# Query and key units of the first mixer: products of 512 columns into two PSUM banks, halves added by VectorE

## The chip, the cores and the metric

One core of one Trainium2 chip runs the whole program. The metric is device time in microseconds (us), the median of several executions; lower is better. Besides these there is one execution recorded by the hardware profiler, from which all rows below come.

## The reference, cut to what matters

The program computes two transformer blocks on 256 tokens of width 1024, in float32. The first is a gated feed-forward, then a mixer, then a second gated feed-forward. The mixer projects its normed input `u` with one wide matrix and splits the columns:

```python
z, xbc, dt_raw, q, k, v, gate_logits = jnp.split(u @ w_in[l], IN_SPLITS, axis=-1)
y_ssd = ssd_branch(z, xbc, dt_raw, ...)      # a chunked scan: 4 groups, 2 chunks of 128 tokens
y_att = diff_attn_branch(q, k, v, ...)       # 8 heads of 2 x 64
merged = gates[:, :, 0] * y_ssd + gates[:, :, 1] * y_att
```

The change concerns the products for `q` and `k` alone (1024 columns each). What is computed stays the same.

## The kernel before, in words

**Precision by parts.** Every float32 product is made of three products of "round" parts. A weight unit is split into an upper part WH (ScalarE, `split_hi`, L487) and a lower part WL = weights - WH (VectorE, `split_lo`, L1082). The input rows are split likewise: XT holds, for each of 8 blocks of 128 input features (`k`), the upper part of the 256 tokens (XTH) and beside it the lower part (XTL), so that `XT[:, k]` is 512 columns. `parts` (L1797) issues WH x XTH, WL x XTH and WH x XTL, all added into one PSUM region.

**Units.** Weights come in units of 128 x 2048 values through a ring of 5 slots, loaded by the SyncE queue, which waits for TensorE to be done with the unit 5 earlier (`w_used`). One query or key unit is 256 columns of the weight. Its 256 output features are the PSUM rows, as two blocks `f` of 128 features, and the 256 tokens the columns. `channels` (L1803) makes for each `f` and `k` three products of 256 columns, 48 in a unit, and both blocks lie in one bank of 512 columns. ScalarE copies that bank to QK (L765). There are 8 such units: 0 to 3 are queries, 4 to 7 keys. The text calls them u0 to u7. They are followed by 4 units for `v` (u8 to u11, rows of tokens, products of 512 columns) and the first gate units (u12, u13).

**Banks.** PSUM has 8 banks: ACC is banks 0 to 3, TOP banks 4 to 7. u0 goes to bank 0, u1 to u7 in turn to 4 and 5 (`q_bank`, L374). Bank 2 takes the C x B products of the scan, bank 3 its outputs, bank 6 its states.

**The order around the change** is written out by hand. The scan runs in steps r = 0 to 8 (loops at L2080 for TensorE, L1406 for VectorE, L776 for ScalarE), and units are put between its products: one unit a step, two in steps 2, 4, 6 and 8 (`beside`, L345). u0 stands before the loop.

- TensorE in step r: the product C x B (L2086), then, from r = 1, the state product (L2098 or L2101) and the 8 output products of the step before (L2104), which wait for VectorE's decay matrix of that step (`ssd_m`, L2102), then the step's units (`qkv`, L2060). So u1 is in step 0, u2 in step 1, u3 and u4 in step 2, u5 in step 3, u6 and u7 in step 4, u8 in step 5. Unit n (n >= 2) waits until unit n-2 is out of its bank (`qkv_kept`, L2068).
- VectorE in step r: scaled inputs XDT (L1414) and in even steps XDEC (L1416), waiting for TensorE's outputs of the step before (`ssd_y`); the sums and the gating of Y (L1423 to L1430); the masked product CBM (L1433); the decay matrix times CBM (L1437), which TensorE awaits; then a wait for ScalarE's row factors (`y_rms`, L1439) and the normed output (L1440); then the step's `split_lo`, one or two.
- ScalarE in step r: 8 Relu and one Exp for the next decay matrix (L783, L786), the state copy (L791), the square of Y after VectorE's L1430 and L1437 (L794), Ln and Exp (L499, L500), then for each unit of the step a `split_hi` and the copy of that unit to QK (L765).

**The same scheme elsewhere.** The feed-forward's gate and up units are already computed as the change does it: `block` (L1865) makes 8 products WH x XT of 512 columns (L1870) and 8 products WL x XTH of 256 columns (L1873) into the right half of the same bank. ScalarE copies the right halves of two banks (L540), and VectorE adds the left halves (L1133).

Of the kernel before, what the change touches and what calls it, by code (L numbers as in the profile page):

```python
# [7 lines left out]
ALU = mybir.AluOpType  # L8
ACT = mybir.ActivationFunctionType
# [6 lines left out]
P = 128  # L16
D = 1024
KD = D // P
NT = 2
TOK = NT * P  # L20
# [169 lines left out]
def program(nc, w, out):  # L190
    with ExitStack() as ctx:
# [83 lines left out]
        def head_sm(q):  # L275
# [34 lines left out]
        end_half, last_half = sem("last_unit_first_columns"), sem("last_rows_halves")  # L310
        conv_1, conv_done, conv_silu, x_turned, x_kept = map(
            sem, ("conv_first_tap", "conv_done", "conv_silu", "x_turned", "x_kept"))
        dt_raw, z_kept, qkv_kept = map(sem, ("dt_raw", "z_kept", "qkv_kept"))
        dt_low, dt_sum, dt_turned, beside_lo = map(sem, ("dt_low_kept", "dt_sum", "dt_turned", "beside_unit_half"))
        cum_kept, cum_stored, cum_spread = sem("cum_rows_kept"), sem("cum_rows_stored"), [
            sem(f"cum_rows_spread{n}") for n in range(2)]
# [54 lines left out]
        def z_bank(n, t):  # L371
            return (2 if n == 1 else 4) + t

        def q_bank(n):  # L374
            return 5 - n % 2 if n else 0

        def v_bank(n, t):
            return ((0, 1), (7, 5))[n][t]


        def slot(c):
            return c % RING
# [99 lines left out]
        def _(act):  # L482
# [271 lines left out]
            def qkv(u):  # L754
                n = u - U_QKV
                split_hi()
                if n == 13:
                    for t in range(NT):
                        chunk_tile(U_GATE0, U_GATE0 + 1, t)
                        nc.scalar.activation(BUF1[:, t, 0:512], PS[gate_bank(0, t)][:], ACT.Copy).then_inc(gate0_kept, 1)  # L760
                elif n == 12:
                    pass
                elif n < 8:
                    act.wait_ge(w_used, u + 1)
                    nc.scalar.activation(QK[:, 2 * (n % 4):2 * (n % 4) + 2, n // 4, :],  # L765
                                         PS[q_bank(n)][:].rearrange("p (f t) -> p f t", f=2),
                                         ACT.Copy).then_inc(qkv_kept, 1)
                elif n % 2:
                    for t in range(NT):
                        chunk_tile(u - 1, u, t)  # L770
                        nc.scalar.activation(V[:, t, (n - 9) * 256:(n - 7) * 256], PS[v_bank(n // 2 - 4, t)][:],
                                             ACT.Copy).then_inc(qkv_kept, 1)

            qkv(U_QKV)
            u = U_QKV + 1
# [300 lines left out]
        def _(dve):  # L1076
# [5 lines left out]
            def split_lo():  # L1082

                c = next(splits, None)
                if c is None:
                    return
                s, n = slot(c), WIDTH.get(c, UNIT)
                dve.wait_ge(w_hi, c + 1)
                tt(WL[:, s, 0:n], RAW[:, s, 0:n], WH[:, s, 0:n].bitcast(F32), ALU.subtract).then_inc(w_lo, 1)  # L1089
# [312 lines left out]
            def heads_bc(ap):  # L1402
                return ap.unsqueeze(2).to_broadcast([P, HPG, SSD_P])

            split_lo()
            for r in range(9):  # L1406
                if r < 8:
                    g, c = divmod(r, 2)
                    xs = BUF1[:, c, g * GW:(g + 1) * GW]
                    hs = slice(c * 32 + g * HPG, c * 32 + (g + 1) * HPG)  # L1410

                    if r:
                        dve.wait_ge(ssd_y, r)
                    own.link(tt(by_head(XDT), by_head(xs), heads_bc(DT[:, 2, hs]), ALU.mult))  # L1414
                    if c == 0:
                        tt(by_head(XDEC), by_head(XDT), heads_bc(EX[:, 1, c, g * HPG:(g + 1) * HPG]),  # L1416
                           ALU.mult).then_inc(xdec_ok, 1)
                if r:
                    n = r - 1
                    g, c = divmod(n, 2)  # L1420
                    dve.wait_ge(skip_ok, r)
                    dve.wait_ge(ssd_y, r)
                    own.link(tt(Y, PS[3][:], Y, ALU.add))  # L1423
                    if c:
                        dve.wait_ge(ssd_st, r)
                        own.link(tt(by_head(T1), by_head(PS[6][:]),
                                    heads_bc(EX[:, 0, c, g * HPG:(g + 1) * HPG]), ALU.mult))
                        own.link(tt(Y, Y, T1, ALU.add))
                    zs = BUF2[:, c, g * GW:(g + 1) * GW]
                    tt(Y, Y, zs, ALU.mult).then_inc(y_gated, 1)  # L1430
                if r < 8:
                    dve.wait_ge(ssd_cb, r + 1)
                    tt(CBM[:], PS[2][:, 0:P], UPTO, ALU.mult).then_inc(ssd_cbm, 1)  # L1433
                    dve.wait_ge(ssd_cbm, r + 1)
                    dve.wait_ge(ssd_e, r + 1)
                    E = DECAY[r % 2]
                    tt(E, E, CBM[:].unsqueeze(1).to_broadcast([P, HPG, P]), ALU.mult).then_inc(ssd_m, 1)  # L1437
                if r:
                    dve.wait_ge(y_rms, r)  # L1439
                    stt(zs, Y, RS[:, 4:5], GAIN[:, g0(n) * GW:(g0(n) + 1) * GW], ALU.mult, ALU.mult).then_inc(ys_ok, 1)  # L1440
                else:
                    def g0(n):
                        return n // 2
                for _u in range(beside(r)):
                    if r == 8 and _u:
                        kt_lo(0)
                    split_lo()


            slopes = [2.0 ** (-8.0 * (h + 1) / DA_HEADS) for h in range(DA_HEADS)]  # L1450
# [254 lines left out]
        def _(pe):  # L1705
# [97 lines left out]
            def channels(c, bank, between=None):  # L1803

                s = slot(c)
                pe.wait_ge(w_lo, c + 1)
                for f in range(2):
                    if f and between:
                        between()
                    for k in range(KD):  # L1810
                        ws = slice(k * 256 + f * P, k * 256 + (f + 1) * P)
                        ins = parts(PS[bank][:, f * TOK:(f + 1) * TOK], WH[:, s, ws], WL[:, s, ws],
                                    XTH[:, k, :], XTL[:, k, :], k == 0, k == KD - 1)
                ins.then_inc(w_used, 1)
# [245 lines left out]
            def qkv(u):  # L2060
                n = u - U_QKV
                if n < 8:
                    if n == 0:
                        pe.wait_ge(conv_done, 11)
                    elif n == 1:
                        pe.wait_ge(z_kept, 8)
                    else:
                        pe.wait_ge(qkv_kept, n - 1)  # L2068
                    channels(u, q_bank(n))
                elif n % 2 == 0:  # L2070
                    v = n // 2 - 4
                    first_half(u, (v_bank(v, 0), v_bank(v, 1)), lambda t: pe.wait_ge(qkv_kept, 7) if v else pe.wait_ge(conv_done, 12))
                else:
                    second_half(u, (v_bank(n // 2 - 4, 0), v_bank(n // 2 - 4, 1)))

# [4 lines left out]
            for r in range(9):  # L2080
                if r < 8:
                    g, c = divmod(r, 2)
                    if r:
                        pe.wait_ge(ssd_cbm, r)

                    mm(PS[2][:, 0:P], BT[:, g, c * P:(c + 1) * P], CT[:, g, c * P:(c + 1) * P], start=True,  # L2086
                       stop=True).then_inc(ssd_cb, 1)
                if r:
                    n = r - 1
                    g, c = divmod(n, 2)  # L2090

                    if n:
                        pe.wait_ge(y_gated, n)
                    pe.wait_ge(cums_exp, 1)
                    pe.wait_ge(cum_cols, 1)
                    if c == 0:
                        pe.wait_ge(xdec_ok, n // 2 + 1)
                        mm(PS[6][:], B0[:, g * P:(g + 1) * P], XDEC, start=True, stop=True).then_inc(ssd_st, 1)  # L2098
                    else:
                        pe.wait_ge(state_ok, n // 2 + 1)  # L2100
                        mm(PS[6][:], CT[:, g, P:TOK], STATE, start=True, stop=True).then_inc(ssd_st, 1)  # L2101
                    pe.wait_ge(ssd_m, r)  # L2102
                    for e in range(HPG):
                        ins = mm(PS[3][:, e * SSD_P:(e + 1) * SSD_P], DECAY[n % 2][:, e, :], XDT[:, e * SSD_P:(e + 1) * SSD_P],  # L2104
                                 start=True, stop=True)
                    ins.then_inc(ssd_y, 1)
                for _u in range(beside(r)):
                    if u < U_GATE0:
                        qkv(u)
                    elif u == U_GATE0:  # L2110
                        first_half(u, (4, 0), lambda t: pe.wait_ge(qkv_kept, 8 + t))
                        pe.wait_ge(qkv_kept, 12)
                        turn_rows(0, BUF2, 0)
                    else:
                        second_half(u, (4, 0))
                    u += 1
# [324 lines left out]
```

## Time and profile before

| what | us |
|---|---|
| runs (3): median, lowest, highest | 1111.6, 1111.05, 1112.52 |
| the profiled execution's own time | 1111.03 |
| its span, first to last instruction | 1109.3 |
| stretch from u0 to the last step of the scan | 318.5 to 421 of the span |
| granted TensorE clock, mean | 1.000 |

All times in rows are us from the start of the span, and durations in them are us unless marked ns. PE is TensorE's products, PEld its weight loads, DVE VectorE, ACT ScalarE. Products overlap: one of 256 columns has a duration of 0.28 and the next begins 0.12 later, so what a stretch of TensorE work costs is read from starts.

### The profile page before, as it was taken

To read this page: it belongs to the slowest core of one execution; us is meant where nothing else is said; L and a number is where in the kernel's file an instruction comes from. 1 tells how busy PE (TensorE), PEld (TensorE's weight loads), DVE (VectorE), ACT (ScalarE), POOL (GpSimd) and SP (SyncE) were. 2 spreads that over 40 slices of the span, in tenths; PEclk is the share of its full clock that TensorE was granted. 3 is DMA by queue.
4 is the path that set the end of the run, shared out by engine and by line. 5 is a ranking of instruction groups with operands and counts; after the bars stand their busy time and mean duration, and the time that the engine had idled before them with its cause. 6 is when DMAs were issued, how large, how long until landed. Compare 5 with 4: busy or idle time off the path is not lost.

```text
span 1109.3 us, 14767 instructions
## 1 busy us (share of the span) xinstructions
PE 1094.5 (99%) x6036; PEld 934.9 (84%) x6036; DVE 770.2 (69%) x896; ACT 619.2 (56%) x883; POOL 36.5 (3%) x66
## 2 busy tenths in 40 slices
PE   7999999999999999999999999999999999999997
PEld 6888888899999987788888888888977778888886
DVE  5766667587767778868768666675784577766664
ACT  7544445564577756655455454456776636444443
POOL 0000000000001100000000000000021100000000
PEclk9999999999999999999999999999999999999999
DMA  9755554755566545345465555545643445555550
GB/s 314 250 192 189 190 191 151 237 168 195 181 189 201 172 152 209 122 155 198 163 219 190 192 188 190 191 150 179 208 137 131 171 152 190 190 189 190 190 190 38
DMA packets 131666, 202.27 MB, mean 182 GB/s; under 512 B 5088, under 2 KB 98144, under 8 KB 131344
## 3 DMA queue, kind: packets, MB, share of 16 engines
q1 hardware_dynamic: 127920, 189.56, 52.2%
q0 software_dynamic: 2672, 10.65, 2.8%
q10 hardware_dynamic: 1008, 1.12, 0.3%
q8 instruction: 48, 0.79, 0.3%
q14 instruction: 18, 0.15, 0.0%
HBM read 200.24 MB, written 1.08 MB: 181 GB/s over the span
## 4 chain that ended last, share of the span: by engine, by line
PE 91%; DVE 4%; ACT 3%; DMA 1%; issue 1%; ACTq 0%; DVEq 0%
PE TOP L1870 20%; PE ACC L1799 13%; PE ACC L1801 13%; PE ACC L1800 13%; PE TOP L1873 10%; PE TOP L1799 4%; PE TOP L1801 4%; PE TOP L1800 4%; ACT WH L494 1%; DVE WL L1089 1%; PE ACC L2104 1%; PE TOP L1715 1%; DMA RAW<-in_w_in 1%; PE TOP L1938 0%; PE TOP L2278 0%
## 5 line engine op out<-in xcount | busy, mean ns | idle before, releaser
L1089 DVE TENSOR_TENSOR WL<-RAW,WH 128x2048 fp32r<-128x2048 f32 (+3 forms) x177 | 400.0, 2264 | 112.5 <-ACT WH L494 111.9
L494 ACT ACTIVATE WH<-RAW 128x2048 fp32r<-128x2048 f32 (+1 forms) x179 | 337.6, 1890 | 80.4 <-DMA RAW<-in_ffn_w_gate 29.4
L1870 PE MATMUL TOP<-XT,WH 128*128 128x512 f32 x960 | 239.9, 392 | 0.0
L1870 PEld LDWEIGHTS TOP<-XT,WH 128*128 128x128 f32 x960 | 174.3, 189 | 32.4
L1799 PE MATMUL ACC<-WH,KTH 128*128 128x512 f32 (+1 forms) x452 | 178.7, 395 | 0.9 <-DVE KTL L1661 0.8
L1800 PE MATMUL ACC<-WL,KTH 128*128 128x512 f32 (+1 forms) x452 | 175.7, 389 | 0.0
L1801 PE MATMUL ACC<-WH,KTL 128*128 128x512 f32 (+1 forms) x452 | 175.6, 389 | 0.0
L1873 PEld LDWEIGHTS TOP<-XT,WL 128*128 128x128 f32 x960 | 131.0, 190 | 9.4
L1873 PE MATMUL TOP<-XT,WL 128*128 128x256 f32 x960 | 133.8, 282 | 0.0
L540 ACT ACTIVATE SCR<-TOP 128x512 f32<-128x512 f32 x60 | 35.8, 597 | 160.4 <-PE TOP L1873 160.4
L1799 PEld LDWEIGHTS ACC<-WH,KTH 128*128 128x128 f32 x452 | 85.0, 188 | 18.3 <-DVE KTL L1661 1.3
L1801 PEld LDWEIGHTS ACC<-WH,KTL 128*128 128x128 f32 x452 | 84.8, 188 | 17.9
L1800 PEld LDWEIGHTS ACC<-WL,KTH 128*128 128x128 f32 x452 | 85.1, 188 | 15.3
L1133 DVE TENSOR_TENSOR SCR<-TOP,SCR 128x512 f32<-128x512 f32 x60 | 41.4, 691 | 74.5 <-ACT SCR L540 74.5
L1799 PE MATMUL TOP<-WH,XT 128*128 128x512 f32 (+1 forms) x184 | 74.1, 403 | 2.3 <-DVE WL L1295 1.9
L1801 PE MATMUL TOP<-WH,XT 128*128 128x512 f32 (+1 forms) x184 | 71.9, 391 | 0.0
L1800 PE MATMUL TOP<-WL,XT 128*128 128x512 f32 (+1 forms) x184 | 71.8, 390 | 0.0
L1799 PE MATMUL ACC<-XT,WH 128*128 128x256 f32 x208 | 59.3, 285 | 0.0
L1800 PE MATMUL ACC<-XT,WH 128*128 128x256 f32 x208 | 58.8, 283 | 0.0
L1801 PE MATMUL ACC<-XT,WL 128*128 128x256 f32 x208 | 58.8, 283 | 0.0
L1799 PE MATMUL ACC<-WH,XT 128*128 128x512 f32 x144 | 58.4, 405 | 0.1
L1801 PE MATMUL ACC<-WH,XT 128*128 128x512 f32 x144 | 56.3, 391 | 0.0
(308 smaller groups left out, 1446.9 us busy)
## 6 DMA issues: line engine op xcount, KB each, us to landing
RAW<-in_w_in SPq DMA_DIRECT2D x50, 1024.0 KB, 5.2
RAW<-in_ffn_w_down SPq DMA_DIRECT2D x22, 1024.0 KB, 4.9
RAW<-in_ffn_w_gate SPq DMA_DIRECT2D x20, 1024.0 KB, 5.3
RAW<-in_ffn_w_up SPq DMA_DIRECT2D x20, 1024.0 KB, 5.4
RAW<-in_w_down SPq DMA_DIRECT2D x11, 1024.0 KB, 4.9
RAW<-in_w_gate SPq DMA_DIRECT2D x10, 1024.0 KB, 5.4
RAW<-in_w_up SPq DMA_DIRECT2D x10, 1024.0 KB, 5.3
RAW<-in_ssd_w_branch SPq DMA_DIRECT2D x8, 1024.0 KB, 5.0
```

What stands on the lines that cost most here:

```text
L494: nc.scalar.activation(WH[:, s, 0:n], RAW[:, s, 0:n], ACT.Copy).then_inc(w_hi, 1)
L540: nc.scalar.activation(LOW[n], TOP[:, bank:bank + 2, TOK:2 * TOK], ACT.Copy).then_inc(low_kept, 1)
L1089: tt(WL[:, s, 0:n], RAW[:, s, 0:n], WH[:, s, 0:n].bitcast(F32), ALU.subtract).then_inc(w_lo, 1)
L1133: tt(by_block(dst), TOP[:, bank:bank + 2, 0:TOK], LOW[n], ALU.add).then_inc((gate_sum, up_sum)[n], 1)
L1715: ins = nc.tensor.transpose(PS[6 + q][:, k * P:(k + 1) * P], XN[:, t, j * P:(j + 1) * P], IDENT)
L1799: mm(ps, stat_hi, mov_hi, start=first, stop=False)
L1800: mm(ps, stat_hi, mov_lo, start=False, stop=False)
L1801: return mm(ps, stat_lo, mov_hi, start=False, stop=last)
L1870: mm(PS[bank], WH[:, slot(c), ws], XT[:, k, :, :].rearrange("p u t -> p (u t)"), start=k == 0, stop=False)
L1873: ins = mm(PS[bank][:, TOK:2 * TOK], WL[:, slot(c), ws], XTH[:, k, :], start=False, stop=k == KD - 1)
L2104: ins = mm(PS[3][:, e * SSD_P:(e + 1) * SSD_P], DECAY[n % 2][:, e, :], XDT[:, e * SSD_P:(e + 1) * SSD_P], start=True, stop=True)
```

## The change

Units u1 to u7 no longer go through `channels`. Each is now two blocks of 8 products of 512 columns (WH against upper and lower rows side by side) and 8 products of 256 columns (WL against the upper rows, into the right half). A block has a bank of its own, so a unit has two: banks 4 and 5 for odd units, banks 0 and 1 for even ones. u0 stays as it was. ScalarE copies the right halves to QK and signals `qk_low`. A new VectorE instruction, `qk_sum`, adds the left halves in place and signals `qk_kept`, on which unit n+2 waits. `qk_sum` stands at these places of VectorE's order: for u1, u2, u4, u5, u7 in steps 1 to 5 right behind the decay matrix (L1437), for u3 and u6 at the end of steps 2 and 4, behind both `split_lo`. The waits of u2, of the first `v` unit and of the first gate unit are adapted to the new banks and semaphores.

```diff
-        def q_bank(n):
-            return 5 - n % 2 if n else 0
+        def q_banks(n):
+            return TOP[:, 0:2, :] if n % 2 else ACC[:, 0:2, :]
...
                     act.wait_ge(w_used, u + 1)
-                    nc.scalar.activation(QK[:, 2 * (n % 4):2 * (n % 4) + 2, n // 4, :],
-                                         PS[q_bank(n)][:].rearrange("p (f t) -> p f t", f=2),
-                                         ACT.Copy).then_inc(qkv_kept, 1)
+                    dst = QK[:, 2 * (n % 4):2 * (n % 4) + 2, n // 4, :]
+                    if n:
+                        nc.scalar.activation(dst, q_banks(n)[:, :, TOK:2 * TOK], ACT.Copy).then_inc(qk_low, 1)
+                    else:
+                        nc.scalar.activation(dst, PS[0][:].rearrange("p (f t) -> p f t", f=2), ACT.Copy).then_inc(qk_kept, 1)
...
+            def qk_sum(n):
+
+                dve.wait_ge(qk_low, n)
+                dst = QK[:, 2 * (n % 4):2 * (n % 4) + 2, n // 4, :]
+                tt(dst, q_banks(n)[:, :, 0:TOK], dst, ALU.add).then_inc(qk_kept, 1)
...
                     tt(E, E, CBM[:].unsqueeze(1).to_broadcast([P, HPG, P]), ALU.mult).then_inc(ssd_m, 1)
+                if 1 <= r <= 5:
+
+                    qk_sum((1, 2, 4, 5, 7)[r - 1])
                 if r:
                     dve.wait_ge(y_rms, r)
...
                     split_lo()
+                if r in (2, 4):
+                    qk_sum(r + 1 if r == 2 else 6)
...
                     if n == 0:
                         pe.wait_ge(conv_done, 11)
-                    elif n == 1:
+                        channels(u, 0)
+                        return
+                    if n == 1:
                         pe.wait_ge(z_kept, 8)
                     else:
-                        pe.wait_ge(qkv_kept, n - 1)
-                    channels(u, q_bank(n))
+                        pe.wait_ge(qk_kept, n - 1)
+                        if n == 2:
+                            pe.wait_ge(conv_done, 12)
+                    pe.wait_ge(w_lo, u + 1)
+                    for f in range(2):
+                        ps = q_banks(n)[:, f, :]
+                        blocks = [slice(k * 256 + f * P, k * 256 + (f + 1) * P) for k in range(KD)]
+                        for k, ws in enumerate(blocks):
+                            mm(ps, WH[:, slot(u), ws], XT[:, k, :, :].rearrange("p u t -> p (u t)"), start=k == 0, stop=False)
+                        for k, ws in enumerate(blocks):
+                            ins = mm(ps[:, TOK:2 * TOK], WL[:, slot(u), ws], XTH[:, k, :], start=False, stop=k == KD - 1)
+                    ins.then_inc(w_used, 1)
                 elif n % 2 == 0:
                     v = n // 2 - 4
-                    first_half(u, (v_bank(v, 0), v_bank(v, 1)), lambda t: pe.wait_ge(qkv_kept, 7) if v else pe.wait_ge(conv_done, 12))
+                    first_half(u, (v_bank(v, 0), v_bank(v, 1)), lambda t: pe.wait_ge(qk_kept, 7 + v))
...
-                        first_half(u, (4, 0), lambda t: pe.wait_ge(qkv_kept, 8 + t))
-                        pe.wait_ge(qkv_kept, 12)
+                        first_half(u, (4, 0), lambda t: pe.wait_ge(v_kept, 1) if t else pe.wait_ge(qk_kept, 8))
+                        pe.wait_ge(v_kept, 4)
```

## Rows read from the trace of the kernel before

**Rows 1.** The page: busy time, granted clock in 40 slices, and the chain by engine.

```profile
PE 1094.5 (99%) x6036; PEld 934.9 (84%) x6036; DVE 770.2 (69%) x896; ACT 619.2 (56%) x883; POOL 36.5 (3%) x66
...
PEclk9999999999999999999999999999999999999999
...
PE 91%; DVE 4%; ACT 3%; DMA 1%; issue 1%; ACTq 0%; DVEq 0%
```

**Rows 2.** Waits of TensorE's weight loads: waiter, engine waited for, total, times, longest.

```profile
PEld TOP L2128 <- DVE SCR L1484: 2.5, 7, 1.0
...
PEld ACC L1799 <- DVE KTL L1661: 1.3, 1, 1.3
...
PEld ACC L2104 <- DVE SCR L1437: 0.8, 1, 0.8
```

**Rows 3.** Timeline of TensorE, 333 to 380: starts of units and scan products.

```profile
333.34 0.37 PE L1799 MATMUL TOP<-XT,WH 128*128 128x256 f32 x1
...
339.18 0.39 PE L2086 MATMUL ACC<-XN 128*128 128x128 f32 x2
...
341.96 0.36 PE L1799 MATMUL TOP<-XT,WH 128*128 128x256 f32 x1
...
347.79 0.28 PE L1799 MATMUL TOP<-XT,WH 128*128 128x256 f32 x1
...
353.55 0.39 PE L2086 MATMUL ACC<-XN 128*128 128x128 f32 x2
...
356.33 0.36 PE L1799 MATMUL TOP<-XT,WH 128*128 128x256 f32 x1
...
376.54 0.39 PE L2086 MATMUL ACC<-XN 128*128 128x128 f32 x2
...
379.32 0.48 PE L1799 MATMUL ACC<-WH,XT 128*128 128x512 f32 x1
```

**Rows 4.** Timeline of TensorE, 122 to 134: four feed-forward blocks.

```profile
122.78 1.98 PE L1870 MATMUL TOP<-XT,WH 128*128 128x512 f32 x8
124.60 1.11 PE L1873 MATMUL TOP<-XT,WL 128*128 128x256 f32 x8
...
133.93 0.40 PE L1799 MATMUL ACC<-WH,KTH 128*128 128x512 f32 x1
```

**Rows 5.** The page's groups: ScalarE's copy and VectorE's sum of feed-forward halves.

```profile
L540 ACT ACTIVATE SCR<-TOP 128x512 f32<-128x512 f32 x60 | 35.8, 597 | 160.4 <-PE TOP L1873 160.4
...
L1133 DVE TENSOR_TENSOR SCR<-TOP,SCR 128x512 f32<-128x512 f32 x60 | 41.4, 691 | 74.5 <-ACT SCR L540 74.5
```

**Rows 6.** Timeline of VectorE, steps 2 to 5 of the scan.

```profile
347.68 1.23 DVE L1437 TENSOR_TENSOR SCR<-SCR,CBM 128x1024 f32<-128x1024 f32 x1
350.23 0.75 DVE L1440 SCALAR_TENSOR_TENSOR BUF<-SCAN,RS,GAIN 128x512 f32<-128x512 f32 x1 [1.32 <-ACT RS L500]
352.18 4.57 DVE L1089 TENSOR_TENSOR WL<-RAW,WH 128x2048 fp32r<-128x2048 f32 x2 [1.20 <-ACT WH L494]
356.67 0.68 DVE L1414 TENSOR_TENSOR SCAN<-BUF,DT 128x512 f32<-128x512 f32 x1
...
361.87 0.75 DVE L1440 SCALAR_TENSOR_TENSOR BUF<-SCAN,RS,GAIN 128x512 f32<-128x512 f32 x1 [1.60 <-ACT RS L500]
...
366.02 0.68 DVE L1414 TENSOR_TENSOR SCAN<-BUF,DT 128x512 f32<-128x512 f32 x1
...
370.44 1.23 DVE L1437 TENSOR_TENSOR SCR<-SCR,CBM 128x1024 f32<-128x1024 f32 x1
...
379.55 0.69 DVE L1414 TENSOR_TENSOR SCAN<-BUF,DT 128x512 f32<-128x512 f32 x1
```

**Rows 7.** Timeline of ScalarE: the copies of u2 and u4 to QK.

```profile
340.92 0.58 ACT L765 ACTIVATE QK<-TOP 128x512 f32<-128x512 f32 x1
...
354.33 0.59 ACT L765 ACTIVATE QK<-TOP 128x512 f32<-128x512 f32 x1
```

**Rows 8.** The chain that ended last: where it leaves TensorE and comes back.

```profile
379.55 0.70 DVE SCAN L1414
...
428.75 0.55 PE TOP L2128 x3
```

More of the change, by code:

```diff
@@ L312, in program @@
             sem, ("conv_first_tap", "conv_done", "conv_silu", "x_turned", "x_kept"))
-        dt_raw, z_kept, qkv_kept = map(sem, ("dt_raw", "z_kept", "qkv_kept"))
+        dt_raw, z_kept, qk_low, qk_kept, v_kept = map(sem, ("dt_raw", "z_kept", "qk_low_kept", "qk_kept", "v_kept"))
         dt_low, dt_sum, dt_turned, beside_lo = map(sem, ("dt_low_kept", "dt_sum", "dt_turned", "beside_unit_half"))
@@ L771, in qkv @@
                         nc.scalar.activation(V[:, t, (n - 9) * 256:(n - 7) * 256], PS[v_bank(n // 2 - 4, t)][:],
-                                             ACT.Copy).then_inc(qkv_kept, 1)
+                                             ACT.Copy).then_inc(v_kept, 1)
             qkv(U_QKV)
```

## The prediction, made before the changed kernel ran

> **What bounds the kernel.** I read the page first, then TensorE's waits, then the timelines of the stretch that changes. TensorE is busy 99% of the span, at full clock in all 40 slices, and holds 91% of the chain that ended last [rows 1]. In the scan stretch (318 to 421) it waits once, 0.8 us for the first decay matrix, and next, 1.0 us, for the first attention probabilities [rows 2]. So fewer TensorE microseconds look like fewer microseconds of program. The second reading is the chain: it leaves TensorE at 379.55 for VectorE's XDT of step 5 and is back only at 428.75, at that 1.0 us wait [rows 8]. In between VectorE and ScalarE set the pace, and TensorE fills the time with 1 us to spare. What arrives at the end is what happens to the XDT of step 5.
>
> **Price of a unit.** u3 took 347.79 - 341.96 = 5.83, u4 behind it 353.55 - 347.79 = 5.76, which is 48 products of 0.12; the 0.07 is a start behind small products [rows 3]. The new form is in the trace: four feed-forward blocks from 122.78 to 133.93, 11.15 for four, 5.58 for the two of a unit [rows 4]. With the 0.07 a unit costs 5.65, so 0.18 is saved, and 7 units would give 1.3.
>
> The columns are the same (48 x 256 = 16 x 512 + 16 x 256), so all that is saved is what each product costs beside its columns. The Trainium skill (TensorE: Matmul & The Clock Gate, "Back-to-back issue gap") gives N / 2.4 + 2.5 ns for an isolated stream, by which a unit would save only 0.03 us and seven 0.2; it also says that this formula ignores weight loads. The trace's 0.12 a product of 256 is above the rule's 0.109, and the measured 5.58 goes into my sum.
>
> **Price of the sums.** VectorE gets seven additions of 128x512 from PSUM, 0.69 each by the same operation in the feed-forward [rows 5]. Five stand right behind the decay matrix, where VectorE sits idle 1.32 for the row factors (1.60 in step 3) [rows 6]: they cost VectorE nothing while ScalarE is no earlier. Two (u3, u6) stand ahead of the next XDT, 0.6 each unless XDT waits for TensorE anyway. ScalarE's copy keeps its size: 0.60 for two half banks, 0.58 now [rows 5, 7]. No DMA, no POOL work is added. A unit's `w_used` comes later where TensorE is later, and with it the load of the unit five later, whose split stands a whole step or more ahead of its use.
>
> **The new wait.** Before, a bank was free once ScalarE had copied it: u2's copy began at 340.92 [rows 7], and u4, needing that bank, began at 347.79 without a wait. Now u4 needs the sum of u2, and that is queued on VectorE behind the whole scalar work of step 2, behind the decay matrix at 347.68, 1.23 long, ended 348.91 [rows 6]. Behind the waiting u4 on TensorE's queue stand C x B, the state and the output products of step 3, and VectorE's XDT waits for those. Step by step:
>
> 1. u1: TensorE already waits 0.8 for the first decay matrix [rows 2], so its 0.18 only lengthens that wait: nothing. u2 begins at 333.34 as before.
> 2. u2 and u3 save 0.18 each: u3 ends at 347.79 - 0.37 = 347.42.
> 3. u4 waits for the sum of u2: 348.91 + 0.69 = 349.60, restart 0.05 later, 349.65. **Stall 2.2.** It ends 5.65 later, at 355.30.
> 4. C x B, state and outputs: 356.33 - 353.55 = 2.78 [rows 3]. TensorE is at 358.08, 1.75 later than before. The sum of u3 (behind the splits that end at 356.67, so done at 357.4) no longer delays u5, and XDT of step 3 starts at about 358.2, taking 0.1 to 0.15 behind the last product, against 356.67.
> 5. VectorE from XDT to XDT: 366.02 - 356.67 = 9.35. So XDT of step 4 is at 367.55, its decay matrix 4.42 later [rows 6], 371.97, ends 373.20, the sum of u5 373.89.
> 6. TensorE: 358.08 + 5.65 (u5) + 2.78 + 5.65 (u6) = 372.16, and u7 needs the sum of u5: 373.94. **Stall 1.8.** The saving of u5 and u6 is swallowed here. u7 ends at 379.59, the outputs at 382.37.
> 7. XDT of step 5 starts at 382.5 instead of 379.55: 2.95 later. The sum of u6 is done near 381.6, in its shadow.
>
> In 5 the 9.35 holds the idle of 1.60 which other steps have as 1.32 [rows 6]; without that 0.28 the shift is 2.67. I take 2.8. From step 5 on nothing of the change is left but the sum of u7, in idle time; the chain carries 2.8 to 428.75 and TensorE, packed from there, to the end. Net: 2.8 lost, the 1.3 of savings all inside waits.
>
> Against the profiled execution: 1111.03 + 2.8 = 1113.8. That execution lies 0.6 under the median of the runs, so on the median 1111.6 + 2.8 = **1114.4** (0.25% slower). About 0.2%, 2.2 us, is what a measurement of this kernel can tell from no change. The bounds: restart after a wait between 0.05 and, with the first weight load exposed, 0.2, twice; XDT chain 2.67 or 2.95; so 2.6 to 3.3 for this case.
>
> **Rivals.**
>
> A. *The sums come in time.* If u2's sum were done before 347.4 and u5's before TensorE asks, TensorE would do seven units in 1.3 less. It would need VectorE 2.2 ahead of where the rows have it, or products of the new form slower by as much. Even then the gain does not arrive: XDT of steps 3 and 5 started at 356.67 and 379.55, 0.3 and 0.2 after TensorE was free for it [rows 3, 6], VectorE's chain paces 379.55 to 428.75, and the sums of u3 and u6 stand ahead of those XDTs. So 0 to +1.3, or, if these two find slack as well, down to -0.3: 1111.3 to 1112.9, not slower by the bound. For it: VectorE is busy 69%. Against it: the order, in which the sum is behind a decay matrix that ends 1.1 after u4 began. It decides when VectorE's step-2 decay matrix ends before 346.7. Chance 0.15, its halfway cases (one stall of the two) included.
>
> B. *The stalls cost the clock.* TensorE's idle times after its start were 1.3 at most, with the clock granted in full in all slices [rows 1, 2]; now 2.2 and 1.8 come within 25 us, a case no row here shows. If the clock fell from its level of 2.4 GHz to that of 1.2 GHz, the work behind a stall would take twice as long: for one unit 5.65 more, so 1120; bounds 0 and 11 for both. Chance 0.05. The Trainium skill (TensorE: Matmul & The Clock Gate, "HAM oscillation — how this bites in real kernels") warns of a clock that drops again after idle gaps in the stream; its gaps are longer than these, so its rule leaves the clock alone here.
>
> C. *The full saving of 1.3 arrives*, 1110.3, or 1111.4 by the skill's formula above. It would need the wait at 428.75 to follow TensorE and not VectorE, against rows 8. Chance 0.03.
>
> **How the numbers follow.** Forecast 0.77, A 0.15, B 0.05, C 0.03. Of the forecast's 0.77 a tenth may fall under 2.2 (measurement, a stall cut by an earlier sum). Slower by over 0.2%: 0.77 x 0.89 + 0.05 = 0.73. Within 0.2%: 0.09 + 0.15 = 0.24. Faster: 0.03. Range: from 1112.4 (upper half of A) to 1116.0 (forecast 2.6 to 3.3, with the scatter of the runs, 1.5, on top); B, C and most of A lie outside.
>
> **What the changed profile would show.** Right: two waits of TensorE's weight loads for the new `tt` line, about 2.2 near 347.4 and 1.5 to 1.8 near 372; u3 shorter by 0.18; XDT of step 3 near 358.2 and of step 5 near 382.3; the first decay-matrix wait grown from 0.8 to 1.0; the wait of 1.0 near 428 kept, moved by 2.8; VectorE's idle time before L1440 shrunk to about 0.6 where a sum stands ahead. Wrong: XDT of step 5 at 380 or earlier (A), granted clock under 1.00 in a window behind a stall (B), or new waits for the sums of u3 or u6.

## The result, and the profile after

The changed kernel takes 1114.68 us (median of 12 executions, 1113.57 to 1116.5) against 1111.22 before (12 executions, 1110.95 to 1112.52): ratio 1.0034, 95% interval 1.0026 to 1.0042, **slower by 3.5**. The profiled execution took 1114.05 with a span of 1112.4, 3.0 over the one before. One of the 76 executions of the kernel before, among the 33 beside e1 to e4, took 1551.63 at a mean clock of 0.656; it shifts no median.

The page of the changed kernel, in the lines of [rows 1]. TensorE has a little less work and a smaller share, and its share of the chain is 4 points smaller, VectorE's 2 and ScalarE's 1 larger:

```profile
PE 1093.0 (98%) x5924; PEld 928.3 (83%) x5924; DVE 774.3 (70%) x903; ACT 619.3 (56%) x883; POOL 36.4 (3%) x66
...
PE 87%; DVE 6%; ACT 4%; issue 1%; DMA 1%; ACTq 0%; DVEq 0%
```

The waits of TensorE's weight loads, to set beside [rows 2]. The second and third are new, for the added `tt` (L1411), ahead of u4 and u7; so is the last, for the masked product CBM:

```profile
PEld TOP L2153 <- DVE SCR L1497: 2.6, 7, 1.0
...
PEld ACC L2091 <- DVE QK L1411: 2.1, 1, 2.1
...
PEld TOP L2091 <- DVE QK L1411: 1.8, 1, 1.8
...
PEld ACC L2129 <- DVE SCR L1445: 0.8, 1, 0.8
...
PEld ACC L2111 <- DVE CBM L1441: 0.3, 1, 0.3
```

TensorE's timeline over the first stall, beside [rows 3]. Each unit is now two pairs of lines (L2091, L2093). u3's last 8 products start at 346.20, and the next could start 0.95 later, at 347.15; u4 begins at 349.24, and C x B at 354.93:

```profile
341.48 2.10 PE L2091 MATMUL TOP<-XT,WH 128*128 128x512 f32 x8
...
346.20 1.11 PE L2093 MATMUL TOP<-XT,WL 128*128 128x256 f32 x8
349.24 2.11 PE L2091 MATMUL ACC<-XT,WH 128*128 128x512 f32 x8 [1.93 <-DVE QK L1411]
...
354.93 0.39 PE L2111 MATMUL ACC<-XN 128*128 128x128 f32 x2
```

VectorE's timeline, beside [rows 6]. The sum of u2 starts at 348.50, as soon as the decay matrix lets it, and ends at 349.18; u4 begins 0.06 later. XDT of steps 3 and 5 (L1422) now waits for TensorE:

```profile
347.36 1.22 DVE L1445 TENSOR_TENSOR SCR<-SCR,CBM 128x1024 f32<-128x1024 f32 x1
348.50 0.68 DVE L1411 TENSOR_TENSOR QK<-ACC,QK 128x512 f32<-128x512 f32 x1
349.90 0.75 DVE L1451 SCALAR_TENSOR_TENSOR BUF<-SCAN,RS,GAIN 128x512 f32<-128x512 f32 x1 [0.72 <-ACT RS L500]
...
357.95 0.69 DVE L1422 TENSOR_TENSOR SCAN<-BUF,DT 128x512 f32<-128x512 f32 x1 [0.92 <-PE ACC L2129]
...
363.15 0.75 DVE L1451 SCALAR_TENSOR_TENSOR BUF<-SCAN,RS,GAIN 128x512 f32<-128x512 f32 x1 [1.00 <-ACT RS L500]
...
367.31 0.69 DVE L1422 TENSOR_TENSOR SCAN<-BUF,DT 128x512 f32<-128x512 f32 x1
...
382.33 0.69 DVE L1422 TENSOR_TENSOR SCAN<-BUF,DT 128x512 f32<-128x512 f32 x1 [0.93 <-PE ACC L2129]
```

This trace lies 0.31 earlier than the one before (u0 begins at 318.15 here and at 318.46 there). So XDT of step 5 moved by 382.33 + 0.31 - 379.55 = 3.09, and the first attention transposes, which [rows 8] have at 428.75, by 3.08:

```profile
318.15 0.28 PE L1812 MATMUL ACC<-XT,WH 128*128 128x256 f32 x1
...
431.52 0.55 PE L2153 MATMUL TOP<-TAB,SCR 128*128 128x128 f32 x3 [0.56 <-DVE SCR L1497]
```

That is the whole 3.0 of the two profiled executions. The distance between these two products, from u0 to the first attention head, is free of what scatters elsewhere in the program. It is 110.29 before and 113.37 after, and below it is called **the stretch** and given for every kernel. It repeats well: two more profiles of the changed kernel (f1, g4) have 113.35 and 113.34. The kernel before has one profile only.

### The profile page after: what moved, and what is told of

Same layout as the page of the kernel before. It is cut to its first block, busy times and chain, and to the rows that moved or that the text cites. A ratio compares the mean times of both kernels' runs of the same rounds, so it can differ in the third digit from the quotient of the medians.

```text
span 1112.4 us, 14550 instructions
## 1 busy us (share of the span) xinstructions
PE 1093.0 (98%) x5924; PEld 928.3 (83%) x5924; DVE 774.3 (70%) x903; ACT 619.3 (56%) x883; POOL 36.4 (3%) x66
## 3 DMA queue, kind: packets, MB, share of 16 engines
HBM read 200.24 MB, written 1.08 MB: 181 GB/s over the span
## 4 chain that ended last, share of the span: by engine, by line
PE 87%; DVE 6%; ACT 4%; issue 1%; DMA 1%; ACTq 0%; DVEq 0%
PE TOP L1883 20%; PE ACC L1812 13%; PE ACC L1814 13%; PE ACC L1813 13%; PE TOP L1886 10%; PE TOP L1812 3%; PE TOP L1814 3%; PE TOP L1813 3%; ACT WH L494 2%; DVE WL L1091 2%; DVE SCR L1445 1%; PE TOP L1728 1%; DMA RAW<-in_w_in 1%; PE TOP L2318 1%; DVE SCAN L1431 1%
```

## The experiments

Twelve runs were made. Where a time is given against "before", that is the median of the kernel before, run beside it on the same chip: 1111.32 for e1 to e4, 1111.13 for f1 to f4, 1110.96 for g1 to g4.

### e1: the two stalling sums moved ahead

```diff
+                if r in (2, 4):
+                    qk_sum({2: 2, 4: 5}[r])
                 if r < 8:
                     g, c = divmod(r, 2)
...
-                if 1 <= r <= 5:
-                    qk_sum((1, 2, 4, 5, 7)[r - 1])
+                if r in (1, 3, 5):
+                    qk_sum({1: 1, 3: 4, 5: 7}[r])
```

> The changed kernel, with the sums of u2 and u5 at the head of steps 2 and 4, ahead of XDT. The theory that VectorE's chain of steps paces this stretch: the 2.1 stall of u4 and the 1.8 stall of u7 vanish, but each moved sum pushes its step back by 0.6, and the sums of u3 and u6 behind the splits push the next XDT back by 0.6 more, so XDT of step 5 is 2.4 later than in the kernel before. The waits of TensorE reappear at u5 (about 2.2, for the sum of u3) and at u8 (about 1.5, for the sum of u6). Time: before plus 2.4, that is 0.5 under the changed kernel. The rival, that the two stalls are the whole loss: no waits for sums, before minus 1.3.

Measured: 1113.51, that is before + 2.2, ratio 1.0022 (1.0013 to 1.0031); stretch 112.57, before + 2.28. The stalls at u4 and u7 are gone and two others are there (TensorE's waits in e1):

```profile
PEld TOP L2092 <- DVE QK L1411: 2.1, 1, 2.1
...
PEld ACC L1813 <- DVE WL L1091: 1.4, 1, 1.4
```

The first is u5's. The second is u8's, ending at 382.37. The profile names the split (ended 381.65), but the sum of u6 behind it ended at 382.25, so it is the sum that was waited for. VectorE's rows of e1 show why little is gained: it works through, with the sum of u3 between the splits and XDT.

```profile
353.12 4.57 DVE L1091 TENSOR_TENSOR WL<-RAW,WH 128x2048 fp32r<-128x2048 f32 x2 [1.20 <-ACT WH L494]
357.61 0.69 DVE L1411 TENSOR_TENSOR QK<-TOP,QK 128x512 f32<-128x512 f32 x1
358.21 0.68 DVE L1424 TENSOR_TENSOR SCAN<-BUF,DT 128x512 f32<-128x512 f32 x1
```

Taking both stalls away brought back 0.8 of 3.1 in the stretch. The rival "the two stalls are the whole loss" falls.

### e2: u4 and u7 in the old form, in bank 7

The lines that adapt ScalarE's copy and the other waits are left out here.

```diff
+                    elif n in (4, 7):
+                        if n == 4:
+                            pe.wait_ge(x_kept, 9)
+                        else:
+                            pe.wait_ge(qk_one, 1)
+                        channels(u, 7)
+                        return
...
-                if 1 <= r <= 5:
-                    qk_sum((1, 2, 4, 5, 7)[r - 1])
+                if r in (1, 2, 4):
+                    qk_sum({1: 1, 2: 2, 4: 5}[r])
```

> The changed kernel, with u4 and u7 in the old form in bank 7, so that neither waits for a sum and only five sums are left. Chain theory: the sums of u3 and u6 still stand between the splits and the next XDT and cost 0.6 each; u5 waits about 1.4 for the sum of u3 and u8 about 0.8 for that of u6; XDT of step 5 is 1.2 later than before. Time: before plus 1.2. The rival, that the two stalls are the whole loss: before minus 0.7.

Measured: 1112.3, before + 1.0, ratio 1.0009 (1.0000 to 1.0018); stretch 111.37, before + 1.08. TensorE waits 1.3 at u5 and 0.7 at u8 (as in e1, the profile names the split there and the sum of u6 comes right behind it):

```profile
PEld TOP L2099 <- DVE QK L1413: 1.3, 1, 1.3
...
PEld ACC L1813 <- DVE WL L1093: 0.7, 1, 0.7
```

So the sums of u3 and u6 cost the chain of steps 0.5 each by their place alone, without any stall at u4 or u7.

### e3: the kernel before, with ScalarE's square at once

```diff
                     act.wait_ge(y_gated, n + 1)
-                    act.wait_ge(ssd_m, min(r + 1, 8)) if r < 8 else None
```

> The kernel before, with ScalarE's square of Y no longer waiting for the decay matrix of the step (only for the gated Y), so that the row factors are there when VectorE is done with that matrix. Chain theory: VectorE's idle 1.3 ahead of L1440 and the later splits shrink by over 1 a step, VectorE runs ahead and waits for TensorE instead, and TensorE's wait of 1.0 at 428.75 goes: before minus 0.9. The rival, that TensorE alone paces the stretch or that another wait takes the place at once: no change, within 0.2.

Measured: 1111.09, before - 0.2, ratio 0.9996 (0.9987 to 1.0005), which is not told from no change; the stretch is 109.85, 0.44 less. VectorE did get ahead. From 325 to 421 its waits for ScalarE's upper parts of the weights are nearly as before (12.0 against 12.8). The wait for row factors, 10.8 in eight waits in the kernel before (first line), is 1.3 in one in e3, and waits for TensorE have come in its place (second and third line):

```profile
DVE BUF L1440 <- ACT RS L500: 10.8, 8, 1.6
...
DVE SCAN L1413 <- PE ACC L2103: 8.1, 6, 2.4
DVE BUF L1439 <- ACT RS L500: 1.3, 1, 1.3
```

But TensorE's idle time before the first attention head fell only from 1.0 to 0.6. In e3 VectorE waits 1.18 for TensorE's own scores of that head before its softmax starts, and the softmax takes longer than the work put beside it. My expectation had taken the whole 1.0 for VectorE's lateness; by the two profiles, 0.44 of it was.

### e4: the same, and the sums of u2 and u5 inside their steps

```diff
                            ALU.mult).then_inc(xdec_ok, 1)
+                if r in (2, 4):
+                    qk_sum({2: 2, 4: 5}[r])
...
-                if 1 <= r <= 5:
-                    qk_sum((1, 2, 4, 5, 7)[r - 1])
+                if r in (1, 3, 5):
+                    qk_sum({1: 1, 3: 4, 5: 7}[r])
```

and the line of e3 taken out of the changed kernel.

> The changed kernel with the edit of e3, and with the sums of u2 and u5 behind XDEC of steps 2 and 4 instead of behind the decay matrix. Chain theory: VectorE is ahead of TensorE in every step, no unit waits for a sum, the savings of u2 to u7 (1.1) arrive, and the wait of 1.0 at the first attention head goes too: before minus 1.9 to 2.1. The rival, that the sums cost what they take wherever they stand (7 x 0.6): before plus 1 to 2.

Measured: **1109.57**, before - 1.75, ratio 0.9984 (0.9975 to 0.9993); stretch 108.87, 1.42 less, of which 0.98 is below e3. TensorE waits for no sum. The new form of the units then brings the 1.1 that six units were worth, within 0.1. This kernel beats both, by the profiles and by an interval that lies below 1; the gain is smaller than the 0.2% that the prediction takes for the limit of one measurement, so it was measured again (g3).

### f4: the changed kernel with the edit of e3 alone

> The changed kernel with the edit of e3 alone, all sums where the change has them. VectorE's steps now begin when TensorE is done with its outputs, and the decay matrix of steps 2 and 4 ends 1.3 earlier: the two stalls shrink to about 0.85 each, against 0.18 saved in each of u2 to u7. Time: before plus 0.4, 2 us over e4. If the place of the sums didn't matter once VectorE is ahead, it would equal e4, before minus 1.7.

Measured: 1111.84, before + 0.7, ratio 1.0006 (0.9997 to 1.0015), so the time alone isn't told from no change; stretch 111.04, before + 0.75. Two stalls are left:

```profile
PEld ACC L2090 <- DVE QK L1410: 1.1, 1, 1.1
...
PEld TOP L2090 <- DVE QK L1410: 0.9, 1, 0.9
```

Between f4 and e4 nothing differs but the place of two sums, behind the decay matrix or ahead of Y's sums, and it is worth 2.2 in the stretch. With VectorE on the chain of steps, moving the same two sums (e1, to a place just ahead of XDT) is worth 0.8.

### f1, f3, g1, g4: what else made the changed kernel slow

Of the first 12 executions of the changed kernel 7 lay between 1113.57 and 1114.70, and 5 between 1115.62 and 1116.50, with nothing between. Rival B of the prediction, the clock, was open for them. f1, g1 and g4 are the changed kernel unaltered; f3 takes the sum of u2 from its place and puts it behind the normed output (L1440 of the kernel before), so that u4 waits longer.

```diff
+                    if r == 2:
+                        qk_sum(2)
```

> The changed kernel once more, unaltered, beside the next three. Of its 12 executions 7 lay between 1113.6 and 1114.7 and 5 between 1115.6 and 1116.5, the latter with a mean granted clock of 0.997 or 0.998 against 0.998 or 0.999. Theory that a 2.1 stall now and then costs TensorE its full clock: again two groups some 2 apart. Rival, that it was that chip at that hour: one group, 1113.5 to 1114.7.

> The changed kernel, with the sum of u2 moved behind VectorE's normed output L1440 of step 2, so that u4 waits 4.1 to 4.2 instead of 2.1. Chain theory: everything behind it moves by the 2.0, u7 waits 1.8 as before, time = changed kernel + 2.0, that is before + 5. Clock theory: in most runs some us more, with the granted clock at 1.2 GHz in a window behind the stall and a mean clock of 0.997 or under.

f1: 1114.88 (6 executions), in two groups again, three at 1113.73 to 1114.30 and three at 1115.46 to 1115.78. f3: 1118.23, before + 7.1, ratio 1.0063 (1.0050 to 1.0076). Its stretch is 116.98, 3.63 over f1's 113.35, where the longer wait (4.2 against 2.1) accounts for 2.1 and 1.5 is left; all five executions have a mean clock of 0.996 or 0.997. Its profile shows the clock falling. Windows of f3, columns: us; busy (x count) of PE, PEld, DVE, ACT, POOL; granted clock; DMA share; GB/s:

```profile
345.00:350.00 5.00, 2.33 (x15) 1.88 (x13) 3.58 (x6) 1.21 (x5) 0.00 (x0) 1.00 0.33 82
350.00:352.00 2.00, 0.67 (x3) 0.58 (x4) 1.41 (x3) 2.00 (x2) 1.03 (x1) 1.00 0.90 349
352.00:354.00 2.00, 2.00 (x7) 1.51 (x6) 2.00 (x1) 2.00 (x2) 0.00 (x0) 0.51 0.00 0
354.00:356.00 2.00, 2.00 (x11) 1.88 (x10) 2.00 (x2) 0.11 (x1) 0.00 (x0) 0.63 0.00 0
356.00:358.00 2.00, 2.00 (x12) 1.70 (x11) 1.04 (x2) 0.00 (x0) 0.00 (x0) 1.00 0.00 0
```

u4 took 358.56 - 351.33 = 7.23 there, against 5.69 in the changed kernel's first profile.

> The changed kernel unaltered, for its two groups of executions (10 of 18 so far between 1113.6 and 1114.7, 8 between 1115.5 and 1116.5, none between). Clock theory, after the run with the 4.2 stall, where the granted clock stood at 1.2 GHz for 3.4 us behind it: a 2.1 stall does the same now and then, so again two groups, and a profile that falls in the upper one shows a window under 1.00 behind a stall. Rival: the groups come from somewhere else, and the profile of an upper run has full clock at the stalls.

> The changed kernel, one look more for a profile of an execution in the upper group. Clock theory: time above 1115.4 together with a stretch at 1.2 GHz behind u4's or u7's stall, or under 1114.8 with none.

g4 took 1113.67 with full clock at both stalls. g1 had a median of 1115.5, with three of its five executions at 1115.50 to 1115.76, and its profile (1115.76) fell on one of them; a fourth, at 1115.04, lies between the two groups. Windows of g1 over u4's 2.1 stall, and TensorE's timeline:

```profile
346.00:350.00 4.00, 2.07 (x13) 1.73 (x12) 3.53 (x6) 0.84 (x3) 0.00 (x0) 1.00 0.27 50
350.00:352.00 2.00, 2.00 (x7) 1.59 (x6) 0.75 (x1) 1.94 (x3) 0.81 (x1) 0.64 1.04 400
352.00:354.00 2.00, 2.00 (x9) 1.81 (x9) 1.71 (x1) 2.00 (x3) 0.23 (x1) 0.51 0.08 30
354.00:358.00 4.00, 4.00 (x23) 3.19 (x22) 3.48 (x3) 1.43 (x4) 0.00 (x0) 1.00 0.00 0
```

```profile
349.69 3.07 PE L2091 MATMUL ACC<-XT,WH 128*128 128x512 f32 x8 [1.93 <-DVE QK L1411]
352.55 1.74 PE L2093 MATMUL ACC<-XT,WL 128*128 128x256 f32 x8
...
356.92 0.39 PE L2111 MATMUL ACC<-XN 128*128 128x128 f32 x2
```

The 8 products of 512 columns took 2.86 instead of 1.95, u4 took 7.23 instead of 5.69, and the stretch is 114.89 instead of 113.37. **A stall of 2.1 is at times followed by a stretch at 1.2 GHz, at a price of 1.5.** Of all 24 executions of the unaltered changed kernel, 12 had a mean clock of 0.998 or under, with a median of 1115.71 and all but one (1114.31) at 1115.46 or more. The other 12 had 0.999, with a median of 1114.13 and none over 1115.04. The difference, 1.58, is close to that price. The mean clock is no sure sign by itself, since it also counts the time behind the last product: the twelve profiles without a fall among the products have 0.998 to 1.000, the two with one have 0.997. And a fall need not cost its full price. In e1 (stalls of 2.1 and 1.4) eight of the eleven executions had 0.996 to 0.998, five of them 0.997 or less; only one reached 1116.46, and the other seven took 1113.22 to 1114.46. Falls that were hidden behind u8's wait for a sum would explain that, but e1's one profile has full clock, so it isn't shown.

### f2, g2: the stalls filled with idle products

```diff
+                        if n in (4, 7):
+                            pe.wait_ge(x_kept, 9)
+                            pe.wait_ge(w_lo, u + 1)
+                            for _i in range(14 if n == 4 else 12):
+                                mm(PS[7][:, 0:TOK], WH[:, slot(u), 0:P], XTH[:, 0, :], start=True, stop=True)
                         pe.wait_ge(qk_kept, n - 1)
```

These products are extra and their result is not read. g2 has 16 and 14.

> The changed kernel, with 14 idle products of 256 columns into the unused bank 7 ahead of u4's wait and 12 ahead of u7's: they compute nothing that is read, and leave 0.4 of either stall idle. Chain theory: the time is that of the lower group of the changed kernel, 1113.6 to 1114.5, since the stalls are waits for VectorE and not work. Clock theory: the upper group (1115.6 and above) is gone. If the stalls were not what sets the time, 26 products of 0.12 would add 3.1.

> The kernel with filled stalls, now 16 idle products ahead of u4 and 14 ahead of u7, so that TensorE is idle 0.2 or less at either. Clock theory: one group without values above 1115.2, median 0.5 or more under that of the changed kernel in the same call if half of its executions are in the upper group. Rival: the same spread as the changed kernel.

Measured: f2 1114.9, stretch 113.35, as f1's; g2 1114.76, stretch 113.35. What is left of the stalls is 0.5 and 0.4 in f2 and 0.2 at u4 in g2. So 26 or 30 products more cost nothing: the stalls are waits. All ten executions have a mean clock of 0.999, none is low, as the clock theory wants. But the times didn't gather in the lower group. They run from 1113.61 to 1116.20 with a median of 1114.85, 0.7 above the changed kernel's executions at full clock. The gap between two groups that f2 and g2 were to show empty isn't empty, and filling the stalls left f1's median of 1114.88 where it was (g2's is 0.7 under g1's, with five executions each). Where the surplus comes from isn't shown. The profiled executions had full clock in the stretch: of the 1.2 by which the profile of f2 (span 1113.3) exceeds that of g4 (1112.1), 0.6 lies ahead of u0 and 0.6 behind the first attention head. This stays open.

### g3: e4 once more, on another chip

> The kernel of e4 again, on whatever chip this call gets: before minus 1.4 to 1.8, one group, since no stall for a sum is left.

Measured: 1109.57, before - 1.39, ratio 0.9987 (0.9979 to 0.9996); stretch 108.87 as in e4; all 11 executions from 1109.30 to 1110.32. The gain holds.

## Why the prediction was right, point by point

The forecast was 1114.4, slower, and 1114.68 was measured, inside the range of 1112.4 to 1116.0. In units of the profile of before (after + 0.31):

- **Unit price.** 5.65 forecast; 5.67 (u2), 5.67 (u3) and 5.69 (u4) measured. Between e3 and e4 six units saved 0.98, 0.16 each. By the gap formula of the Trainium skill (TensorE: Matmul & The Clock Gate, "Back-to-back issue gap") 16 products fewer at its 2.5 ns are an estimate of 0.04 a unit and 0.3 for seven, not the 0.03 and 0.2 of the prediction; either is far below what was measured. The forecast's sum didn't use it.
- **Step 1 was right in sum, wrong in place.** TensorE's early arrival did not lengthen the wait for the decay matrix (0.8 still). It met C x B of step 1 first, which waits for CBM to be free of the step before: 0.3, new.
- **Step 3.** u4 at 349.65 forecast, 349.55 measured; stall 2.2 and 2.1. The restart behind either sum took 0.06, so the lower bound of 0.05 was right; the 0.2 of the upper bound was not seen.
- **Step 4.** XDT of step 3 at 358.2 forecast, 358.26 measured. The sum of u3 stood in its shadow, as said.
- **Step 5.** XDT to XDT 9.35 forecast, 9.36 measured. The longer idle of step 3 (1.60) came again: 1.00 beside a sum of 0.6. So it belongs to that step and was not a scatter, and my choice of 2.8 between 2.67 and 2.95 should have been 2.95.
- **Steps 6 and 7.** Stall at u7 1.8 and 1.8; XDT of step 5 at 382.5 forecast, 382.64 measured. The shift was 3.09 where I took 2.8.
- **No other part of the program gave anything back.** The shift at step 5 was the shift at the attention (3.08) and of the profiled execution (3.0).
- **The range.** By its own terms its upper end is 1111.6 + 3.3 + 1.5 = 1116.4, not 1116.0; the result lies inside either.
- **Partly luck: the median came within 0.3.** The loss was 3.5 where 2.8 was forecast, 0.3 of that in the chain. But the 1111.6 it was added to, a median of three, was 0.4 above the 1111.22 of twelve executions, and the two errors in part cancel.

**Rival A** was right about what would hold the gain back: with the stalls taken away (e1, e2) the loss was still 2.3 and 1.1, since VectorE's chain of steps was the pace and two sums stand on it. Its "0 to 1.3" for sums in time fits e2, not e1, where the two moved sums add 0.6 each. What I had missed is that one edit takes VectorE off that chain (e3), and then the placing is worth 2.2 (f4 against e4).

**Rival B** had a chance of 0.05 and, by the mean clock, happened in half of the executions, beside the forecast's own mechanism and not in its place; g1 shows the sign that the prediction had named for it. Its price was far too high, 5.65 a stall; the clock came back within the unit, and it cost 1.5. Its ground was also misread. TensorE's waits in the kernel before have one of 2.3 that the prediction passes over:

```profile
PEld TOP L1799 <- DVE WL L1295: 2.3, 1, 2.3
```

It ends at 7.03, in the start of the program, where the products were slow anyway (last section), so it speaks neither for B nor against it.

The Trainium skill (TensorE: Matmul & The Clock Gate, "HAM oscillation — how this bites in real kernels"), as I had read it, left the clock alone at 2.2; the runs show a fall behind 2.1, and the measurement decides. Of the twelve executions of the result, the six with a mean clock of 0.999 have a median of 1114.33. That is 3.1 over 1111.22, the 3.08 of the stretch. The other 0.4 of the 3.5 goes with the six at 0.998 or less. So the chain's loss, forecast 2.8, was 0.3 short, and the clock stood in the sum at nothing. That the clock's falls lift the median isn't shown by an experiment, since without them f2 came out as f1 and g2 0.7 under g1.

**The reading of rows 8** as "1 us to spare" was too coarse: 0.6 of it follows TensorE's own scores and stays whatever VectorE does (e3).

## What to carry to other kernels

An engine at 99% busy doesn't mean that its microseconds are the program's: look at where the chain leaves it, and for how long another engine's sequence sets the starts. When a buffer's release moves from one engine's queue to another's, find the instruction that it is now queued behind and compare its end with the start that it must meet; then ask what the added instruction does to that queue at its own place. Here the loss became a gain only when the engine that set the starts was first freed of a wait (e3) and the added instruction then put ahead of the long work that it had stood behind (e4 against f4). A stall of 2 us on TensorE may cost more than its own length, so price the clock when a change opens one.

## What the runs showed of the hardware that was not expected

The granted clock fell to 1.2 GHz behind single idle times of 2.1 (up to 12 of 24 executions by their mean clock, one seen in a profile) and 4.2 (all five by their mean clock, one seen in a profile). In both profiles TensorE had been busy over 99% of the time from 40 to 345. In the executions without a profile a fall behind u7's 1.8 can't be told from one behind u4's 2.1. The clock fell not in the idle time but 0.7 to 0.9 after the products had started again, and stood at 1.2 GHz for 3.4 in both profiles (worked out from the windows of f3 and g1). In the kernels whose longest stall in this stretch was 1.3 or less (e2, e3, e4, f4 and g3) no execution lay more than 0.9 above its kernel's median. The kernel before, whose longest idle time there is 1.0, had executions 1.3 and 1.1 above theirs (1112.52 and 1112.09, the latter at a mean clock of 1.000), apart from the one named with the result.

At the start of the program the row of the granted clock doesn't tell what the products do. Two pairs of neighbours in the kernel before, all of 512 columns:

```profile
7.62 0.63 PE L1800 MATMUL TOP<-WL,XT 128*128 128x512 f32 x1
8.05 0.63 PE L1801 MATMUL TOP<-WH,XT 128*128 128x512 f32 x1
...
14.92 0.40 PE L1799 MATMUL TOP<-WH,XT 128*128 128x512 f32 x1
15.15 0.40 PE L1800 MATMUL TOP<-WL,XT 128*128 128x512 f32 x1
```

They start 0.43 apart and then 0.23 apart, while the granted clock of both windows is given as 1.00. Over the fourteen profiles the last distance of 0.43 ends between 10.2 and 12.9. The prediction's "full clock in all 40 slices" holds only behind that.
